# Second expert table read from the last column to the first, with PSUM written backwards

## The chip, the cores and the metric

The kernel runs on one core of one Trainium2 chip. The metric is the device time of one execution in microseconds, the median of several runs. TensorE (PE) multiplies, VectorE (DVE) and ScalarE (ACT) do elementwise work, GpSimd (POOL) helps with it, and SyncE (SP) issues the DMA transfers.

## The reference

One decoder layer over 256 tokens of width 1024. After two kinds of attention and an output projection, each token picks experts out of 16,384 by product keys; each expert is a single neuron with a row in the table `peer_u` and a row in the table `peer_v`:

```python
u = u_table[idx_c]
hid = jax.nn.gelu(jnp.einsum('cd,ced->ce', x_c, u), approximate=False)
return jnp.einsum('ce,ced->cd', g_c * hid, v_table[idx_c])
```

The result is added to the residual `h`. A last gate, `h + sigmoid(RMSNorm(h) @ W_g) * (p @ W_ple)`, gives the output.

## The kernel before, in words

The kernel doesn't gather rows of experts. It computes all 16,384 neurons for all 256 tokens as dense products, and the weights of the experts that a token didn't pick are zero. Each table goes through SBUF in 128 chunks of 128 experts x 1024 columns (512 KB), in a ring of four places (`RING`).

Products of fp32 accuracy are made of three products of a shorter format (fp32r): a tensor is split into a rounded part (`_hi`) and what is left (`_lo`), and hi x hi, hi x lo and lo x hi are summed in PSUM.

The first table's stage (about 185 to 577 us) makes the hidden values: `hidden` calls `three` (L1261 to L1263), whose output is 128 experts x 256 tokens. The second table's stage (about 577 to 927 us) is `expert_sum`, which the diff touches. For chunk n = 4i + q:

- SP loads the chunk into `t_raw` (L361) as soon as TensorE has raised `v_used` for the chunk that was in this place.
- ACT rounds it to `t_hi` (L613) and the gated hidden values `slots` to `g_hi` (L687).
- DVE subtracts, which gives `t_lo` (L964) and `g_lo` (L1144).
- TensorE multiplies. For two token tiles (`tt`) and two halves of 512 columns (`w`) it makes the three products L1597, L1599 and L1600, 12 in a chunk, and adds them up in the four PSUM banks 0 to 3 over all 128 chunks. The gates are the stationary operand, the table's rows the moving one.

The work of each engine is written out by hand in its own program, and the engines meet at semaphores. After the last chunk DVE adds the four banks to `h` (L1177), TensorE transposes `h` (L1248) and the last stage makes the gate with products of 512 and of 256 columns (L1640 to L1642).

Two other places bear on the prediction. `running_sum` (L1379 to L1384) has a product whose output leaves out every other 128 columns of a bank:

```python
mm(bank[3 * e + b][:, :].rearrange("p (i t) -> p i t", i=2)[:, :, P:SEQ], ones,
   upper[:, 256 * b:256 * (b + 1)].rearrange("p (i t) -> p i t", i=2), start=False,
```

and `biased` (L872) has DVE read an operand in SBUF from its last column to its first:

```python
in1=skew[:, a:b:2, 0:SEQ - s_from][:, :, ::-1], op0=ALU.mult, op1=ALU.add)
```

L1505 makes the key scores with plain f32 operands, which aren't split.

Of the kernel before, what the change touches and what calls it, by code (L numbers as in the profile page):

```python
# [72 lines left out]
def layer_program(nc, x, first, p_t, rel_bias, bucket_onehot, consts, qk_gain, w_in, w_out, w_query,  # L73
# [5 lines left out]
    with ctx:  # L79
# [11 lines left out]
        def tile(name, shape, offset, dt=f32):  # L91
            return nc.alloc_sbuf_tensor_at(name, shape, dt, offset=offset)
# [76 lines left out]
        t_lo = tile("t_lo", [P, RING, D], ZONE, f32r)  # L169
# [3 lines left out]
        g_hi = tile("g_hi", [P, RING, SEQ], ZONE + 4 * 4096, f32r)  # L173
        g_lo = tile("g_lo", [P, RING, SEQ], ZONE + 4 * 5120, f32r)
        t_hi = tile("t_hi", [P, RING, D], ZONE + 4 * 7168, f32r)
# [12 lines left out]
        bank = [pairs[b // 2][:, 2 * (b % 2):2 * (b % 2) + 2, :, :].rearrange("p a b c -> p (a b c)")  # L188
                for b in range(4)] + [ctx.enter_context(nc.psum_tensor(f"bank{b}", [P, 512], f32))
                                      for b in range(4, 8)]  # L190
# [3 lines left out]
        def xt_half(k, c):  # L194
            return half((4, 5, 6, 7)[c // 2] if k == 2 else (0, 1, 4, 5)[c // 2] if k == 1 else c // 2, c % 2)
# [82 lines left out]
        def u_lo(q, i):  # L278
            return t_lo_pool, RING * i + q + 1
# [964 lines left out]
        def _(pe):  # L1244
            mm = nc.tensor.matmul

            def transpose(src, tt, c, dst):
                return nc.tensor.transpose(dst, src[:, tt, P * c:P * (c + 1)], ident)  # L1248
# [57 lines left out]
            for c in range(DC):  # L1306
# [7 lines left out]
                for tt in range(TT):  # L1314
                    ins = mm(bank[4 + tt][:, :], xt_hi[:, c, P * tt:P * (tt + 1)], w_lo[:, 0, c, :], start=False,
                             stop=(c == DC - 1))
# [7 lines left out]
            for tt in range(TT):  # L1324
                ins = mm(bank[1][:, P * tt:P * (tt + 1)], neg_ones, diag[:, P * tt:P * (tt + 1)], start=True, stop=True)
# [8 lines left out]
            for g in range(8):  # L1334
                for tt in range(TT):
                    ins = nc.tensor.transpose(bank[g // 2][:, 256 * (g % 2) + P * tt:256 * (g % 2) + P * (tt + 1)],
                                              qk_nat[:, tt, 2 * g:2 * g + 2, :].rearrange("p a b -> p (a b)"), ident)
# [8 lines left out]
            for i in range(4):  # L1346
                if i >= 2:
                    pe.wait_ge(columns_out, 2 + i)
                for e in range(2):
                    r = slice(HD * e, HD * (e + 1))  # L1350
                    mm(bank[3 * e + i // 2][:, 256 * (i % 2):256 * (i % 2) + 256], qkt_s[r, 4 + i, 0:P], qkt_s[r, i, :],
                       start=(i % 2 == 0), stop=True, skip_group_check=True)
                for e in range(2):
                    r = slice(HD * e, HD * (e + 1))
                    ins = mm(bank[3 * e + 2][:, P * i:P * (i + 1)], qkt_s[r, 4 + i, P:SEQ], qkt_s[r, i, P:SEQ],
                             start=(i == 0), stop=True, skip_group_check=True)
# [41 lines left out]
            for hh in range(NH):  # L1398
# [3 lines left out]
                ins = nc.tensor.transpose(bank[weight_banks[hh // 4]][:, P * (hh % 4):P * (hh % 4 + 1)], s0[:, hh, :], ident)  # L1402
# [5 lines left out]
            for tt in range(TT):  # L1408
                for hh in range(NH):
                    e, i = hh % 2, hh // 2  # L1410
                    cols = slice(512 + HD * hh, 512 + HD * (hh + 1))
                    dst = bank[4 + tt][:, HD * hh:HD * (hh + 1)]
                    c = 256 * i + P * tt
                    ins = mm(dst, sb_w[:, e, c:c + P], v_all[:, 0, cols], start=True, stop=(tt == 0))
                    if tt:
                        ins = mm(dst, sb_w[:, e, 1024 + P * i:1024 + P * (i + 1)], v_all[:, 1, cols], start=False,
                                 stop=True)
# [3 lines left out]
            for hh in range(NH):  # L1421
                ins = mm(bank[2][:, HD * hh:HD * (hh + 1)], probs_t[:, hh // 4, P * (hh % 4):P * (hh % 4 + 1)],
                         v_all[:, 0, HD * hh:HD * (hh + 1)], start=True, stop=True)
# [3 lines left out]
            for hh in range(NH):  # L1427
                if hh % 4 == 0:
                    pe.wait_ge(s_exp, 3 + hh // 4)
                for ss in range(2):  # L1430
                    c = 256 * (hh % 2) + P * ss
                    ins = nc.tensor.transpose(bank[weight_banks[2 + hh // 2]][:, c:c + P], s1[:, hh, P * ss:P * (ss + 1)], ident)
# [10 lines left out]
            for hh in range(NH):  # L1443
# [5 lines left out]
                for ss in range(2):  # L1449
                    c = 256 * (hh % 2) + P * ss  # L1450
                    ins = mm(bank[3][:, HD * hh:HD * (hh + 1)], probs_t[:, place, c:c + P],
                             v_all[:, ss, HD * hh:HD * (hh + 1)], start=(ss == 0), stop=(ss == 1))
# [34 lines left out]
            for tt in range(TT):  # L1487
                pe.wait_ge(xs_ready, tt + 1)
                for c in range(DC):
                    ins = transpose(xs, tt, c, xt_half(2, c)[:, P * tt:P * (tt + 1)])  # L1490
# [53 lines left out]
            for q in range(2):  # L1544
                for tt in range(TT):
                    ins = nc.tensor.transpose(bank[q][:, P * tt:P * (tt + 1)], pick[:, tt, q, :], ident)
                ins.then_inc(pick_t_done, 1)
            pe.wait_ge(picks_ready, 1)
            for tt in range(TT):
                ins = nc.tensor.transpose(bank[2][:, P * tt:P * (tt + 1)],  # L1550
                                          gate[:, tt, :, :].rearrange("p a b -> p (a b)"), ident)
# [33 lines left out]
            def expert_sum(q, i, first=False, tiles=(0, 1)):  # L1585
                if 0 in tiles:
                    if first and q < LEAD:
                        pe.wait_ge(*u_lo(q, N_KEYS // RING))
                    else:
                        pe.wait_ge(t_lo_ready, RING * i + q - LEAD + 1)  # L1590
                    pe.wait_ge(g_lo_ready, RING * i + q + 1)
                for tt in tiles:
                    t = slice(P * tt, P * (tt + 1))
                    for w in range(2):
                        d = slice(512 * w, 512 * (w + 1))
                        dst = bank[2 * tt + w][:, :]
                        mm(dst, g_hi[:, q, t], t_hi[:, q, d], start=first and q == 0, stop=False,  # L1597
                           skip_group_check=True)
                        mm(dst, g_hi[:, q, t], t_lo[:, q, d], start=False, stop=False, skip_group_check=True)  # L1599
                        ins = mm(dst, g_lo[:, q, t], t_hi[:, q, d], start=False, stop=True,  # L1600
                                 skip_group_check=True)
                if 1 in tiles:
                    ins.then_inc(v_used, 1)
                return ins
# [10 lines left out]
            for q in range(RING):  # L1615
                expert_sum(q, 0, first=True)
            with pe.Fori(1, N_KEYS // RING - 1) as i:
                for q in range(RING):
                    expert_sum(q, i)
            for q in range(RING - 2):  # L1620
                expert_sum(q, N_KEYS // RING - 1)
            for q in range(RING - 2, RING):
                ins = expert_sum(q, N_KEYS // RING - 1, tiles=(0,))
# [6 lines left out]
            for u, (tt, d0, width, b) in enumerate(END_PARTS):  # L1630
                t, d = slice(P * tt, P * (tt + 1)), slice(d0, d0 + width)
                dst = bank[b][:, 0:width]
# [4 lines left out]
                for c in range(DC):  # L1637
                    if c % 2 == 0:
# [3 lines left out]
                    ins = mm(dst, xt_lo[:, c, t], wg_hi[:, c, d], start=False, stop=(c == DC - 1),  # L1642
                             skip_group_check=True)
# [66 lines left out]
```

## Time and profile before

| what | value |
|---|---|
| median of 3 runs | 954.15 us (953.89 to 954.45) |
| span of the profiled execution | 954.3 us |
| own time of the profiled execution | the page gives none beside the span |
| TensorE busy | 946.7 us (99%) |
| VectorE, ScalarE, GpSimd busy | 689.4, 614.5, 334.2 us |
| clock granted to TensorE | full in every slice |

The span reaches from the first to the last instruction of one execution. Busy times of TensorE count a product from its start to its modelled end, and products overlap, so that the distance from one start to the next says more of their price than their duration.

### The profile page before, as it was taken

Reading aid. Unit: us, or ns where it says so; the run is one execution under the profiler, and the core shown is the slowest. Engines: PE = TensorE matmul, PEld = TensorE weight load, DVE = VectorE, ACT = ScalarE, POOL = GpSimd, SP = SyncE. Lnnn points to the kernel's source line nnn. Section 1 sums busy time; section 2 is a strip of 40 time slices with the busy share of each in tenths; the row PEclk is TensorE's granted clock in tenths of the full one; section 3 lists DMA queues with packets and bytes.
Section 4 is the critical chain, followed back from the end, with each engine's and each line's share of the span. In section 5 each row is a group of like instructions: output and inputs, shape, how many; then the busy total and the mean of one; then the engine's idle time right before and its main releaser. Section 6 shows DMA issues by size and latency. Waiting matters only on the chain.

```text
span 954.3 us, 19175 instructions
## 1 busy us (share of the span) xinstructions
PE 946.7 (99%) x6220; PEld 863.2 (90%) x6220; DVE 689.4 (72%) x1389; ACT 614.5 (64%) x1039; POOL 334.2 (35%) x148
## 2 busy tenths in 40 slices
PE   9999999999999999999999999999999999999998
PEld 6988889999999999999999998888888888888887
DVE  6648864999987888889888875555555555566763
ACT  6778754456676888888888875544545554556643
POOL 0003500288887777777777772000000000000000
PEclk9999999999999999999999999999999999999999
DMA  9860453055555544444444445555567776655521
GB/s 335 305 257 1 156 214 133 24 177 185 189 180 175 175 161 170 163 167 158 172 160 170 164 167 196 185 193 197 197 229 236 239 244 222 195 197 191 188 105 45
DMA packets 46459, 172.08 MB, mean 180 GB/s; under 512 B 5043, under 2 KB 8668, under 8 KB 44892
## 3 DMA queue, kind: packets, MB, share of 16 engines
q1 hardware_dynamic: 46284, 171.53, 51.9%
q8 instruction: 19, 0.31, 0.1%
q10 hardware_dynamic: 144, 0.15, 0.1%
q14 instruction: 12, 0.10, 0.0%
HBM read 169.55 MB, written 2.11 MB: 180 GB/s over the span
## 4 chain that ended last, share of the span: by engine, by line
PE 88%; ACT 4%; DVE 3%; issue 2%; DMA 2%; POOL 1%; SPq 1%; DVEq 0%; ACTq 0%; POOLq 0%
PE bank L1262 12%; PE bank L1261 12%; PE bank L1263 12%; PE pair L1597 12%; PE pair L1600 12%; PE pair L1599 12%; PE pair L1558 3%; DMA h<-x 1%; PE pair L1295 1%; PE pair L1296 1%; PE pair L1297 1%; PE bank L1295 1%; PE bank L1297 1%; PE bank L1296 1%; PE bank L1642 1%
## 5 line engine op out<-in xcount | busy, mean ns | idle before, releaser
L613 ACT ACTIVATE t_hi<-t_raw 128x1024 fp32r<-128x1024 f32 x256 | 270.3, 1056 | 165.9 <-DMA t_raw<-v_chunks 162.5
L1233 POOL TENSOR_TENSOR t_lo<-t_raw,t_hi 128x1024 fp32r<-128x1024 f32 x130 | 311.9, 2411 | 147.0 <-ACT t_hi L613 147.0
L1262 PE MATMUL bank<-xt_lo,t_hi 128*128 128x256 f32 x1024 | 287.5, 281 | 0.0
L1261 PE MATMUL bank<-xt_hi,t_hi 128*128 128x256 f32 x1024 | 287.0, 280 | 0.2 <-POOL t_lo L1233 0.2
L1263 PE MATMUL bank<-xt_hi,t_lo 128*128 128x256 f32 x1024 | 286.5, 280 | 0.0
L964 DVE TENSOR_TENSOR t_lo<-t_raw,t_hi 128x1024 fp32r<-128x1024 f32 x126 | 154.4, 1226 | 136.5 <-ACT t_hi L613 136.3
L1597 PE MATMUL pair<-t_hi,g_hi 128*128 128x512 f32 x512 | 199.5, 390 | 0.3 <-DVE g_lo L1144 0.3
L1599 PE MATMUL pair<-t_lo,g_hi 128*128 128x512 f32 x512 | 199.2, 389 | 0.0
L1600 PE MATMUL pair<-t_hi,g_lo 128*128 128x512 f32 x512 | 199.2, 389 | 0.0
L1263 PEld LDWEIGHTS bank<-xt_hi,t_lo 128*128 128x128 f32 x1024 | 193.1, 189 | 0.0
L1261 PEld LDWEIGHTS bank<-xt_hi,t_hi 128*128 128x128 f32 x1024 | 192.8, 188 | 0.4 <-POOL t_lo L1233 0.4
L1262 PEld LDWEIGHTS bank<-xt_lo,t_hi 128*128 128x128 f32 x1024 | 192.4, 188 | 0.0
L1597 PEld LDWEIGHTS pair<-t_hi,g_hi 128*128 128x128 f32 x512 | 96.1, 188 | 20.9 <-DVE g_lo L1144 1.3
L1600 PEld LDWEIGHTS pair<-t_hi,g_lo 128*128 128x128 f32 x512 | 96.1, 188 | 20.0
L1599 PEld LDWEIGHTS pair<-t_lo,g_hi 128*128 128x128 f32 x512 | 96.1, 188 | 19.9
L1097 DVE TENSOR_SCALAR hot_j<-bank,pick_t 128x128 fp32r<-128x128 f32 x256 | 87.0, 403 | 0.0
L664 ACT ACTIVATE hot_j<-hot_j,ratio 128x128 fp32r<-128x128 f32 x256 | 82.1, 394 | 0.0
L677 ACT ACTIVATE bank<-bank 128x256 f32<-128x256 f32 x88 | 32.4, 368 | 39.8 <-PE bank L1263 33.1
L1113 DVE TENSOR_TENSOR slots<-slots,bank 128x256 f32 (+1 forms) x88 | 36.4, 414 | 28.7 <-ACT bank L677 28.7
L1144 DVE TENSOR_TENSOR g_lo<-slots,g_hi 128x256 fp32r<-128x256 f32 x128 | 54.4, 425 | 0.6 <-ACT g_hi L687 0.6
L687 ACT ACTIVATE g_hi<-slots 128x256 fp32r (+1 forms) x128 | 51.2, 400 | 0.6 <-DVE slots L1113 0.6
L1107 DVE TENSOR_TENSOR slots<-slots,pair 128x512 f32 (+1 forms) x64 | 44.1, 688 | 7.5
(285 smaller groups left out, 1286.5 us busy)
## 6 DMA issues: line engine op xcount, KB each, us to landing
t_raw<-u_chunks SPq DMA_DIRECT2D x128, 512.0 KB, 3.2
t_raw<-v_chunks SPq DMA_DIRECT2D x128, 512.0 KB, 3.3
w_raw<-w_query SPq DMA_DIRECT2D x4, 2048.0 KB, 8.1
w_raw<-w_in SPq DMA_DIRECT2D x3, 2048.0 KB, 10.4
w_raw<-w_out SPq DMA_DIRECT2D x2, 2048.0 KB, 8.2
wg_raw<-w_gate SPq DMA_DIRECT2D x8, 512.0 KB, 5.2
first_raw<-first SPq DMA_DIRECT2D x7, 384.0 KB, 7.0
w_raw<-w_in SPq DMA_DIRECT2D x4, 512.0 KB, 11.2
```

Of the source, the lines that this page charges most:

```text
L613: nc.scalar.activation(t_hi[:, q % RING, :], t_raw[:, q % RING, :], ACT.Copy).then_inc(t_hi_ready, 1)
L664: ins = nc.scalar.activation(hot_j[:, k, q, 1, :], hot_j[:, k, q, 0, :].bitcast(f32), ACT.Copy, scale=ratio[:, bass.ds(4 * s + q, 1)])
L964: nc.vector.tensor_tensor(t_lo[:, q % RING, :], t_raw[:, q % RING, :], t_hi[:, q % RING, :].bitcast(f32), ALU.subtract).then_inc(t_lo_read ...
L1097: nc.vector.tensor_scalar(hot_j[:, k, q, 0, :], lanes, pick_t[:, 1, bass.ds(t, 1)], pick_t[:, 2, bass.ds(t, 1)], ALU.is_equal, ALU.mult).t ...
L1144: nc.vector.tensor_tensor(g_lo[:, k, :], src, g_hi[:, k, :].bitcast(f32), ALU.subtract).then_inc(g_lo_ready, 1)
L1233: nc.gpsimd.tensor_tensor(t_lo[:, q, :], t_raw[:, q, :], t_hi[:, q, :].bitcast(f32), ALU.subtract).then_inc(t_lo_pool, 1)
L1261: mm(dst, ah, bh, start=(c == 0), stop=False)
L1262: mm(dst, ah, bl, start=False, stop=False)
L1263: ins = mm(dst, al, bh, start=False, stop=(c == n - 1))
L1597: mm(dst, g_hi[:, q, t], t_hi[:, q, d], start=first and q == 0, stop=False, skip_group_check=True)
L1599: mm(dst, g_hi[:, q, t], t_lo[:, q, d], start=False, stop=False, skip_group_check=True)
L1600: ins = mm(dst, g_lo[:, q, t], t_hi[:, q, d], start=False, stop=True, skip_group_check=True)
```

## The change

The three products of `expert_sum` take the columns of the table's half in descending order, and the output bank in descending order too. Each number is added at the same place of PSUM as before; only the order within a product is another.

```diff
                     for w in range(2):
                         d = slice(512 * w, 512 * (w + 1))
-                        dst = bank[2 * tt + w][:, :]
-                        mm(dst, g_hi[:, q, t], t_hi[:, q, d], start=first and q == 0, stop=False,
+                        dst = bank[2 * tt + w][:, ::-1]
+                        mm(dst, g_hi[:, q, t], t_hi[:, q, d][:, ::-1], start=first and q == 0, stop=False,
                            skip_group_check=True)
-                        mm(dst, g_hi[:, q, t], t_lo[:, q, d], start=False, stop=False, skip_group_check=True)
-                        ins = mm(dst, g_lo[:, q, t], t_hi[:, q, d], start=False, stop=True,
+                        mm(dst, g_hi[:, q, t], t_lo[:, q, d][:, ::-1], start=False, stop=False,
+                           skip_group_check=True)
+                        ins = mm(dst, g_lo[:, q, t], t_hi[:, q, d][:, ::-1], start=False, stop=True,
                                  skip_group_check=True)
```

## Rows read from the trace of the kernel before

**Rows 1.** The page: busy time of the engines; granted clock in 40 slices, in tenths.

```profile
PE 946.7 (99%) x6220; PEld 863.2 (90%) x6220; DVE 689.4 (72%) x1389; ACT 614.5 (64%) x1039; POOL 334.2 (35%) x148
...
PEclk9999999999999999999999999999999999999999
```

**Rows 2.** The page: the chain that ended last, by engine, by line.

```profile
PE 88%; ACT 4%; DVE 3%; issue 2%; DMA 2%; POOL 1%; SPq 1%; DVEq 0%; ACTq 0%; POOLq 0%
PE bank L1262 12%; PE bank L1261 12%; PE bank L1263 12%; PE pair L1597 12%; PE pair L1600 12%; PE pair L1599 12%; PE pair L1558 3%; DMA h<-x 1%; PE pair L1295 1%; PE pair L1296 1%; PE pair L1297 1%; PE bank L1295 1%; PE bank L1297 1%; PE bank L1296 1%; PE bank L1642 1%
```

**Rows 3.** The page's groups: busy us, mean ns | idle us before them.

```profile
L1597 PE MATMUL pair<-t_hi,g_hi 128*128 128x512 f32 x512 | 199.5, 390 | 0.3 <-DVE g_lo L1144 0.3
L1599 PE MATMUL pair<-t_lo,g_hi 128*128 128x512 f32 x512 | 199.2, 389 | 0.0
L1600 PE MATMUL pair<-t_hi,g_lo 128*128 128x512 f32 x512 | 199.2, 389 | 0.0
```

**Rows 4.** Timeline of TensorE, second table's stage: start us, duration us, line.

```profile
577.43 0.39 PE L1597 MATMUL pair<-t_hi,g_hi 128*128 128x512 f32 x1
...
700.55 0.39 PE L1597 MATMUL pair<-t_hi,g_hi 128*128 128x512 f32 x1
...
700.77 0.39 PE L1599 MATMUL pair<-t_lo,g_hi 128*128 128x512 f32 x1
...
701.00 0.39 PE L1600 MATMUL pair<-t_hi,g_lo 128*128 128x512 f32 x1
...
701.23 0.39 PE L1597 MATMUL pair<-t_hi,g_hi 128*128 128x512 f32 x1
...
925.13 0.38 PE L1248 MATMUL pair<-cst,h 128*128 128x128 f32 x2
...
925.92 0.47 PE L1597 MATMUL pair<-t_hi,g_hi 128*128 128x512 f32 x1
...
927.15 0.39 PE L1600 MATMUL pair<-t_hi,g_lo 128*128 128x512 f32 x1
```

**Rows 5.** Timeline of TensorE, last stage, two widths.

```profile
937.82 0.39 PE L1640 MATMUL bank<-wg_hi,xt_hi 128*128 128x512 f32 x1
...
939.63 0.39 PE L1642 MATMUL bank<-wg_hi,xt_lo 128*128 128x512 f32 x1
...
945.81 0.28 PE L1641 MATMUL bank<-wg_lo,xt_hi 128*128 128x256 f32 x1
...
946.89 0.28 PE L1641 MATMUL bank<-wg_lo,xt_hi 128*128 128x256 f32 x1
```

**Rows 6.** Timeline of TensorE, plain f32 key scores and what follows.

```profile
181.52 3.73 PE L1505 MATMUL pair<-sk,query 128*128 128x128 f32 x32
185.01 0.36 PE L1261 MATMUL bank<-xt_hi,t_hi 128*128 128x256 f32 x1
```

**Rows 7.** Timeline of TensorE, running sums.

```profile
80.09 0.28 PE L1381 MATMUL pair<-sp_hi,tri_r 128*128 128x256 f32 x1
80.20 0.40 PE L1379 MATMUL pair<-sp_hi,tri_r 128*128 128x512 f32 x1
80.43 0.28 PE L1381 MATMUL pair<-sp_hi,tri_r 128*128 128x256 f32 x1
80.55 0.40 PE L1384 MATMUL pair<-sp_hi,tri_r 128*128 128x512 f32 x1
```

**Rows 8.** Groups of DVE by line and shape, columns as in rows 3.

```profile
L927 DVE SCALAR_TENSOR_TENSOR h<-bank,stats,h 128x512 f32<-128x512 f32 x4 | 2.9, 746 | 0.1
...
L872 DVE SCALAR_TENSOR_TENSOR s<-bank,skew 128x512 f32<-128x512 f32 x4 | 2.6, 684 | 1.3 <-PE bank L1368 1.3
```

**Rows 9.** One stretch: its length; PE, PEld, DVE, ACT, POOL busy; clock, DMA share, GB/s.

```profile
660.00:780.00 120.00, 120.00 (x531) 99.41 (x530) 67.81 (x87) 60.00 (x88) 0.00 (x0) 1.00 0.67 227
```

**Rows 10.** Waits of SP's queue: total us, times, longest us.

```profile
SPq L361 <- PE pair L1600: 255.4, 124, 2.7
```

## The prediction

> **What bounds the kernel now.** I read the page's first part before anything else: TensorE is busy for 946.7 of 954.3 us, and its clock row grants full speed, 2.4 GHz, in all 40 slices [rows 1]. The chain of work that ended last says the same by another road: 88% of the span is TensorE, and three lines of the second table's loop, L1597, L1599 and L1600, hold 12% each, as the three lines of the first table do [rows 2]. So the second table's products are about 36% of the time by the chain, and the change edits these three lines and nothing else.
>
> Next I read that stage alone. The groups of instructions give 512 products of 128x512 on each line, 389 to 390 ns each [rows 3]. That duration is not the price of one: products overlap in the array. The price is the distance between starts. The timeline shows L1597, L1599 and L1600 and the next L1597 starting 0.22 to 0.23 us after each other, with no idle time noted before any of them [rows 4]. Over the stage, from the first L1597 at 577.43 to the last L1600 at 927.15, lie 349.7 us; the eight transposes of h that stand among the last products take 0.8 of them (925.13 to 925.92 in the timeline) [rows 4]. 348.9 us over 1,535 distances is 227.3 ns a product.
>
> What in those 227 ns depends on the columns? The last stage runs the same kind of product in two widths with hardly anything beside it: 512 columns start every 0.227 us (937.82 to 939.63 is 8 distances, 1.81 us), 256 columns every 0.120 us (945.81 to 946.89 is 9 distances, 1.08 us) [rows 5]. The difference, 107 ns for 256 columns, is 0.417 ns a column, one column for each beat of the 2.4 GHz clock; about 13 ns are left that no column pays for. The table stage therefore already runs at one column per beat: 213 + 14 = 227. It also runs at this pace while DMA, ACT and DVE are at work, as the last stage does almost alone, so nobody visibly disturbs its reads.
>
> **The change, part by part.** It removes no instruction, adds none, moves none and adds no wait. 128 table rows x 2 token tiles x 2 halves x 3 products = 1,536 products read their moving operand (t_hi or t_lo) from column 511 down to 0 and write the PSUM bank from 511 down to 0. Both reversed, each number lands where it did, so the DVE additions that read the banks afterwards, and the residual h, are untouched. The stationary operand (g_hi, g_lo) and its load are untouched as well. No queue changes order: DMA issues wait for v_used, which the last product of a row still raises.
>
> So there is one unknown: what a column costs when the addresses of a product go down. No row here shows a product that goes down, so I bound it. The lower bound is nothing: 0.417 ns a column stays, and 1,536 x 0 = 0. A gain would have to come out of the 13 to 14 ns beside the columns; all of it gone would be 1,536 x 13.3 ns = 20.4 us, and since a product of another stage pays the same 13 ns [rows 5] with other tiles, I see nothing in the order of columns that would free it. The upper bound comes from products that already cost more per column: the plain f32 scores of L1505. 32 records of 128 columns start between 181.52 and the next line's start at 185.01, which is 109 ns each, and with the 13 ns taken off 96 ns, 0.75 ns a column; taken with nothing off it is 0.85 [rows 6]. That is about two beats a column. Two beats for the reversed products would cost 512 x 0.417 = 213 ns more each, 1,536 x 213.3 ns = 327.7 us.
>
> The nearest rows favour the lower end. L1381 writes a bank in two runs with 128 columns left out between them, and it has the start distance of an unbroken 256-column product, 0.11 to 0.12 us [rows 7]; a break in the run is no cost by itself. And DVE already reads an operand from its last column to its first: L872 takes skew backwards and needs 684 ns for 512 columns, while L927, the same operation on as many columns going up, needs 746 [rows 8]. Both are neighbours only: the first still goes up inside each run, the second is another engine at more than 1 ns a column, which leaves its memory more time. I take zero for the sum, by the nearer row (same engine, same port), and keep 327.7 us as the other end.
>
> A rule speaks to this. The Trainium skill, "PSUM — Partial Sum Buffer", section Specifications (TRN2), says that PSUM is kept in lines of 8 bytes, two fp32 values, and that an access pattern which isn't contiguous slows matmuls a good deal. Read by the letter, a step of -1 isn't contiguous, and the sum would be the 327.7 us above or more; read by its lines, 511 and 510 share a line as 0 and 1 do, and the sum would be zero. Rows 7 don't decide it, since both runs there are made of whole lines.
>
> Nothing would hide a dearer column. TensorE has no idle time in this stage [rows 4], so every ns goes to the end. The others have room: in 120 us of the stage TensorE is busy for 120.0, DVE for 67.8, ACT for 60.0, DMA for 0.67 of the time [rows 9], and ACT waits for v rows only because the next load waits for TensorE to release a slot (SP's queue waited 255.4 us in total for L1600) [rows 10]. A dearer product gives them more room and changes no order.
>
> The sum: 954.3 + 0 = 954.3 us by the profiled span. The page gives no other time for that execution; the median of the runs is 954.15, 0.15 below, and I predict against it: 954.2. About 0.2%, some 2 us, is what a measurement of this kernel can tell from no change.
>
> **The rivals.**
>
> *Half rate (slower).* The two memories that a product touches hand over or take two fp32 columns in one access only if the second lies above the first; downward each column takes an access, and so two beats. Place: every one of the 1,536 products, in reading, in writing, or both at once (they run side by side, so both cost no more than one). Price: 327.7 us, so 954.2 + 327.7 = 1,281.9 us, and a start distance of 227 + 213 = 440 ns. It decides as soon as a column takes more than one beat. For it: the array takes a column each 0.417 ns and has no slack at all against its ports, so any lost pairing shows in full. Against it: rows 7 and 8. It is also where the letter of the rule in the Trainium skill's "PSUM — Partial Sum Buffer" would end.
>
> *A charge per product.* The descending start costs a bubble about as large as the 13 ns that a product already pays: 1,536 x 13.3 = 20.4 us, 974.6 us. For it: such a charge exists. Against it: L1381, whose starting address and shape differ from its neighbours', pays no more.
>
> *The change does nothing.* If the two reversals are cancelled when the program is put together, since reading and writing in either order is the same product, the time is 954.2 as well. It isn't told apart by the time, only by an experiment with one of them.
>
> **How the numbers follow.** No cost (with cancelled reversals): 0.54. Half rate: 0.36. Charge per product, or anything between it and half rate: 0.05. Four beats: 0.02. Faster: 0.03. The likeliest gives 954.2; its own range is 952.5 to 956. The whole range has to reach to half rate, for without it over 4 in 10 would be left out: 952 to 1,295, the upper end being 1,281.9 with 4% of the 327.7 for what lies beside the columns. Faster by over 0.2%: 0.03; within it: 0.54; slower: 0.36 + 0.05 + 0.02 = 0.43.
>
> **What would show it.** Right: the three lines still start every 227 ns, 349 us from first to last, and the chain gives each 12%. Half rate: starts 440 ns apart, the stage 677 us long, each line about 18% of a span of 1,282, with ACT's and DVE's waits in the stage growing and DMA's share falling by half. A charge: starts 240 ns apart. The prediction would be wrong through one thing only, the price of a descending column on one of TensorE's two ports; which port it is, the time doesn't say.

## The result, and the profile after

The changed kernel takes 964.62 us (median of 4 runs, 964.11 to 964.93) against 954.3 of before (4 runs): ratio 1.0102, 95% interval 1.0090 to 1.0114. It is slower by 10.3 us, about 1%; the number lies inside the stated range of 952 to 1,295 us only because that range had to reach as far as half rate; the likeliest value, 954.2, and its own range, 952.5 to 956, missed it.

First the page of the changed kernel: busy times, granted clock, chain by engine and by line. L1601 is the third product, which was L1600.

```profile
PE 955.8 (99%) x6220; PEld 864.0 (90%) x6220; DVE 678.2 (70%) x1389; ACT 616.1 (64%) x1039; POOL 334.6 (35%) x148
...
PEclk9999999999999999999999999999999999999999
...
PE 91%; ACT 3%; DVE 2%; issue 2%; POOL 1%; DMA 0%; POOLq 0%; ACTq 0%
PE pair L1601 12%; PE pair L1599 12%; PE pair L1597 12%; PE bank L1262 12%; PE bank L1261 12%; PE bank L1263 12%; PE pair L1558 3%; PE pair L1297 1%; PE pair L1295 1%; PE pair L1296 1%; PE bank L1295 1%; PE bank L1297 1%; PE bank L1296 1%; PE bank L1643 1%; PE bank L1641 1%
...
L1597 PE MATMUL pair<-t_hi,g_hi 128*128 128x512 f32 x512 | 203.5, 398 | 0.0
L1599 PE MATMUL pair<-t_lo,g_hi 128*128 128x512 f32 x512 | 203.5, 397 | 0.0
L1601 PE MATMUL pair<-t_hi,g_lo 128*128 128x512 f32 x512 | 203.5, 397 | 0.0
```

Nothing has changed its kind: the same number of instructions, full clock, the same bound, the same three lines with 12% each (answering to [rows 1, 2]). Only the products' duration has grown by 8 ns [rows 3]. The timeline of the changed kernel gives their distance:

```profile
576.87 0.40 PE L1597 MATMUL pair<-t_hi,g_hi 128*128 128x512 f32 x1
...
929.68 0.40 PE L1597 MATMUL pair<-t_hi,g_hi 128*128 128x512 f32 x1
...
933.65 0.40 PE L1601 MATMUL pair<-t_hi,g_lo 128*128 128x512 f32 x1
933.89 0.38 PE L1248 MATMUL pair<-cst,h 128*128 128x128 f32 x2
...
934.68 0.48 PE L1597 MATMUL pair<-t_hi,g_hi 128*128 128x512 f32 x1
...
935.93 0.40 PE L1601 MATMUL pair<-t_hi,g_lo 128*128 128x512 f32 x1
```

From 929.68 to 933.65 are 17 distances in 3.97 us: 233.5 ns, where before had 226 to 227 [rows 4]. The start times that the trace keeps to the nanosecond give 233.3 and 226.7. The stage lasts 935.93 - 576.87 = 359.1 us in place of 349.7. A view that counts products in a fixed stretch tells paces apart well; here it is for 600 to 900 us, before and after (length; PE, PEld, DVE, ACT, POOL busy with the number of instructions; clock, DMA share, GB/s):

```profile
600.00:900.00 300.00, 299.71 (x1322) 247.54 (x1321) 178.27 (x226) 155.94 (x226) 0.00 (x0) 1.00 0.62 210
```

```profile
600.00:900.00 300.00, 300.00 (x1287) 241.66 (x1286) 172.78 (x220) 151.06 (x220) 0.00 (x0) 1.00 0.60 204
```

300 us by 1,322 products is 226.9 ns, by 1,287 it is 233.1. (Such a quotient is rough to some 0.3 ns: the count takes in products that reach over an edge, and the stretch of before holds five longer distances, of 243 to 681 ns.) DVE and ACT do less in the stretch because they have fewer chunks to serve, and SP waits a little longer for TensorE:

```profile
SPq L361 <- PE pair L1601: 264.6, 124, 2.3
```

(255.4 before [rows 10]). So the loss is all in the distance between products: some 6.7 ns x 1,536 = 10.3 us. The spans of the two profiled executions differ by 8.8 us only. Here span and time can be compared: the changed kernel's profiled run took 964.77 us with a span of 963.1, and runs of the kernel before such as 954.56 us had a span of 952.8, so the execution behind the rows of before, with its span of 954.3, was itself some 1.5 us slower than the median.

### The profile page after: what moved, and what is told of

Read it like the earlier page. It is cut to its first block, busy times and chain, and to the rows that moved or that the text cites. A ratio compares the mean times of both kernels' runs of the same rounds, so it can differ in the third digit from the quotient of the medians.

```text
span 963.1 us, 19175 instructions
## 1 busy us (share of the span) xinstructions
PE 955.8 (99%) x6220; PEld 864.0 (90%) x6220; DVE 678.2 (70%) x1389; ACT 616.1 (64%) x1039; POOL 334.6 (35%) x148
## 4 chain that ended last, share of the span: by engine, by line
PE 91%; ACT 3%; DVE 2%; issue 2%; POOL 1%; DMA 0%; POOLq 0%; ACTq 0%
PE pair L1601 12%; PE pair L1599 12%; PE pair L1597 12%; PE bank L1262 12%; PE bank L1261 12%; PE bank L1263 12%; PE pair L1558 3%; PE pair L1297 1%; PE pair L1295 1%; PE pair L1296 1%; PE bank L1295 1%; PE bank L1297 1%; PE bank L1296 1%; PE bank L1643 1%; PE bank L1641 1%
## 5 line engine op out<-in xcount | busy, mean ns | idle before, releaser
L1262 PE MATMUL bank<-xt_lo,t_hi 128*128 128x256 f32 x1024 | 287.4, 281 | 0.0
L1261 PE MATMUL bank<-xt_hi,t_hi 128*128 128x256 f32 x1024 | 287.2, 280 | 0.2 <-POOL t_lo L1233 0.2
L1263 PE MATMUL bank<-xt_hi,t_lo 128*128 128x256 f32 x1024 | 286.5, 280 | 0.0
L1597 PE MATMUL pair<-t_hi,g_hi 128*128 128x512 f32 x512 | 203.5, 398 | 0.0
L1599 PE MATMUL pair<-t_lo,g_hi 128*128 128x512 f32 x512 | 203.5, 397 | 0.0
L1601 PE MATMUL pair<-t_hi,g_lo 128*128 128x512 f32 x512 | 203.5, 397 | 0.0
L1261 PEld LDWEIGHTS bank<-xt_hi,t_hi 128*128 128x128 f32 x1024 | 192.7, 188 | 0.4 <-POOL t_lo L1233 0.4
L1263 PEld LDWEIGHTS bank<-xt_hi,t_lo 128*128 128x128 f32 x1024 | 193.0, 189 | 0.0
L1262 PEld LDWEIGHTS bank<-xt_lo,t_hi 128*128 128x128 f32 x1024 | 192.5, 188 | 0.0
L1601 PEld LDWEIGHTS pair<-t_hi,g_lo 128*128 128x128 f32 x512 | 96.3, 188 | 23.3
L1599 PEld LDWEIGHTS pair<-t_lo,g_hi 128*128 128x128 f32 x512 | 96.3, 188 | 23.1
```

What stands on the lines that cost most here:

```text
L1261: mm(dst, ah, bh, start=(c == 0), stop=False)
L1262: mm(dst, ah, bl, start=False, stop=False)
L1263: ins = mm(dst, al, bh, start=False, stop=(c == n - 1))
L1597: mm(dst, g_hi[:, q, t], t_hi[:, q, d][:, ::-1], start=first and q == 0, stop=False, skip_group_check=True)
L1599: mm(dst, g_hi[:, q, t], t_lo[:, q, d][:, ::-1], start=False, stop=False, skip_group_check=True)
L1601: ins = mm(dst, g_lo[:, q, t], t_hi[:, q, d][:, ::-1], start=False, stop=True, skip_group_check=True)
```

## The experiments

Three theories after the result. D: a descending read costs 6.7 ns by itself. S: the cost lies between the last address of one product and the first of the next. W: it lies between the product's read of the table and the read of the stationary operand (the gates) for the next product. In a measured result the brackets hold the ratio to the kernel before, run beside it, and its 95% interval. In the two runs that turn only one of reading and writing, the host lays each half of the table out mirrored, so that the output stays the same.

**Which port?**

```diff
 read_down:   dst = bank[2 * tt + w][:, :]        t_hi[:, q, d][:, ::-1]   (t_lo alike)
 write_down:  dst = bank[2 * tt + w][:, ::-1]     t_hi[:, q, d]
+both:        v_chunks ... .reshape(N_KEYS, N_KEYS, 2, 512)[..., ::-1]
```

> Only the moving operand is read downward; the PSUM bank is written upward, and the table's halves are mirrored in memory beforehand so that the output is the same. Theory A (the 6.7 ns a product, 1,536 x 6.7 = 10.2 us, arise where the moving operand is read): 964.5 us, the three lines start every 233 ns. Theory B (they arise where PSUM is written): 954.3 us, 227 ns. Theory C (either one alone costs it, both side by side no more): 964.5 here and in the run that only writes downward.

> Only the PSUM bank is written downward, the operand is read upward (halves mirrored in memory). Theory A (reading): 954.3 us, 227 ns a product. Theory B (writing): 964.5 us, 233 ns. Theory C: 964.5.

Measured: 964.38 us (1.0101, 1.0084 to 1.0118) and 954.62 us (1.0001, 0.9992 to 1.0011). The same stretch of read_down, then of write_down:

```profile
600.00:900.00 300.00, 300.00 (x1287) 241.71 (x1286) 172.66 (x219) 151.09 (x220) 0.00 (x0) 1.00 0.60 205
```

```profile
600.00:900.00 300.00, 300.00 (x1325) 248.41 (x1324) 179.04 (x227) 155.92 (x226) 0.00 (x0) 1.00 0.61 211
```

The whole loss comes with the read; writing PSUM downward is free. The Trainium skill's rule that a PSUM pattern which isn't contiguous slows matmuls ("PSUM — Partial Sum Buffer", Specifications (TRN2)) doesn't hold by the letter for a step of -1: 1,325 products in the stretch against 1,322.

**Per product or per column?**

```diff
-                    for w in range(2):
-                        d = slice(512 * w, 512 * (w + 1))
-                        dst = bank[2 * tt + w][:, :]
+                    for w in range(4):
+                        d = slice(256 * w, 256 * (w + 1))
+                        dst = half(2 * tt + w // 2, w % 2)     # quarters_down: [:, ::-1], and t_hi, t_lo too
...                                                            # start only where w is even: two quarters share a bank
```

> Control, nothing downward: the same stage with products of 256 columns, 3,072 in place of 1,536. From rows 5 a 256-column product starts every 120 ns: 3,072 x 120 = 368.6 us in place of 1,536 x 227 = 348.7, so 954.3 + 20 = 974 us whatever the theory.

> The changed kernel with 256-column products, all downward. If the charge is one per product: 3,072 x 6.7 = 20.5 us above the control, about 995 us, starts 126.7 ns apart. If it is a charge per column (10.2 us over the same 786,432 columns): about 984.5 us, starts 123.3 ns apart.

Measured: up 974.96 us (1.0208), as expected; down 969.79 us (1.0157), 5.2 us faster than up, where both theories wanted it slower. The stretch of quarters_up, then of quarters_down:

```profile
600.00:900.00 300.00, 300.00 (x2503) 300.00 (x2502) 167.27 (x214) 146.74 (x213) 0.00 (x0) 1.00 0.58 199
```

```profile
600.00:900.00 300.00, 300.00 (x2534) 299.80 (x2533) 169.58 (x215) 148.29 (x216) 0.00 (x0) 1.00 0.60 202
```

119.9 ns up, 118.4 down. With 256 columns going down gains 1.5 ns, with 512 it loses 6.7. So there is neither a charge for a descending product nor one for a descending column that holds at both widths. What is left is that the 13 ns beside the columns are no constant.

**Where in the product?** middle_down reverses L1599 alone; blocks_down takes four runs of 128 columns in descending order and each run upward; runs_down leaves the runs in order and reverses each.

```diff
 middle_down: mm(dst[:, ::-1], g_hi[:, q, t], t_lo[:, q, d][:, ::-1], ...)     # the other two as before
 blocks_down: t_hi[:, q, d].rearrange("p (b c) -> p b c", b=4)[:, ::-1, :]      # t_lo and dst alike
 runs_down:   t_hi[:, q, d].rearrange("p (b c) -> p b c", b=4)[:, :, ::-1]
```

> Only the second product of each three (L1599, which reads t_lo) goes downward. Theory D (a descending read costs 6.7 ns by itself): the product that goes down takes 233 ns to the next start, the other two 227; 512 x 6.7 = 3.4 us, 957.9 us. Theory S (the cost lies at the change from one product's last address to the next one's first address): here a product that ended at column 511 is followed by one that starts at 511, and one that ended at 0 by one that starts at 0; neither pair stands in the kernel before or in the changed one, so the distances are neither 227 nor 233 and change at two of the three lines. Theory W (the read meets the next weights' read in SBUF): as D for this run.

> Each product takes its four runs of 128 columns in descending order, and each run upward. Theory D (a step of -1): 227 ns, 954.5 us. Theory S (last and first address): the product starts at column 384 and ends at 127, so the distance moves off 227, towards 233 if a start above the end is what costs. Theory W: no firm number; off 227 if the address in the first part of a product decides, since that is when the next weights are loaded.

> The four runs of 128 columns stand in ascending order, and each run goes downward. Theory D: the step of -1 costs at least as much as before, 233 ns or more, 964.5 us or more (four turns in place of one). Theory S: starts at 127 and ends at 384, near to the upward order, 227 ns, 954.5 us. Theory W: between, as the first run is read downward while weights are loaded.

Measured: 958.5 us (1.0038, 1.0024 to 1.0053), 955.23 us (1.0004, 0.9995 to 1.0014) and 965.2 us (1.0112, 1.0095 to 1.0129). The stretch of middle_down, blocks_down and runs_down:

```profile
600.00:900.00 300.00, 299.82 (x1308) 244.97 (x1307) 176.87 (x224) 154.14 (x225) 0.00 (x0) 1.00 0.60 208
```

```profile
600.00:900.00 300.00, 299.58 (x1322) 247.77 (x1321) 178.25 (x226) 156.00 (x227) 0.00 (x0) 1.00 0.60 210
```

```profile
600.00:900.00 300.00, 300.00 (x1285) 241.17 (x1284) 173.43 (x221) 151.07 (x220) 0.00 (x0) 1.00 0.60 205
```

One product of three reversed costs about a third, 3.9 us, and by the start times it is the reversed product's own distance to the next start that grows: L1599 takes 232 or 233 ns, the other two mostly 226 to 228. A product that starts at column 384 and ends at 127 costs nothing while its runs go up, and one that starts at 127 and ends at 384 pays in full when its runs go down. S is out: first and last address don't matter. The order inside a run does, and four descending runs cost no more than one of 512.

**Does the place of the gates matter?** The two gate tiles, which TensorE reads as the stationary operand, are moved by 128 or 64 bytes within the row of each partition; the tables stay.

```diff
-        g_hi = tile("g_hi", [P, RING, SEQ], ZONE + 4 * 4096, f32r)
-        g_lo = tile("g_lo", [P, RING, SEQ], ZONE + 4 * 5120, f32r)
+        g_hi = tile("g_hi", [P, RING, SEQ], ZONE + 4 * 4128, f32r)     # 64 bytes: 4112
+        g_lo = tile("g_lo", [P, RING, SEQ], ZONE + 4 * 5152, f32r)     #           5136
```

> The changed kernel with both gate tiles (the stationary operands) 128 bytes further on in SBUF; the table tiles stay where they are. Theory W (the descending read meets the weights' read in the same part of SBUF): the distance moves off 233 ns, in one direction or the other. Theories D and S know nothing of the weights: 233 ns, 964.5 us.

> The changed kernel with the gate tiles 64 bytes further on in place of 128. Theory W: the place of the weights sets the pace of the downward products, so that it is again another (226.7, 240 or a mixture; 954 to 975 us), and it may differ between executions as with 128 bytes (965.1 and 974.0 us). Theory D: 233.3 ns and 964.5 us in each execution.

> Control for the run with the gates 128 bytes further on: the same shift, all products upward. [...] Theory D (the step of -1 costs, the place of the weights doesn't): 226.7 ns, 954.5 us, and no execution with another pace.

Measured: 128 bytes, down, 965.08 us (1.0107, 1.0090 to 1.0124; five runs: 964.52, 964.82, 965.08, 967.22 and 974.04, of which 974.04 is the profiled one); 64 bytes, down, 965.09 us (1.0113); 128 bytes, up, 964.14 us (1.0102, 1.0085 to 1.0119). The last is the key run: nothing goes downward in it, and it loses as much as the change. The stretch of gates_shifted_down (its execution of 974.04 us), gates_shifted_64_down and gates_shifted_up:

```profile
600.00:900.00 300.00, 300.00 (x1251) 234.69 (x1250) 168.00 (x213) 147.56 (x214) 0.00 (x0) 1.00 0.57 199
```

```profile
600.00:900.00 300.00, 300.00 (x1288) 241.54 (x1287) 172.61 (x219) 151.08 (x220) 0.00 (x0) 1.00 0.60 204
```

```profile
600.00:900.00 300.00, 300.00 (x1291) 242.57 (x1290) 172.75 (x220) 152.04 (x221) 0.00 (x0) 1.00 0.61 205
```

Two timelines show two kinds of loss. First gates_shifted_down, where each product starts exactly 0.24 us after the last; then gates_shifted_up, where the distances are uneven, 0.23 and 0.24:

```profile
700.08 0.40 PE L1599 MATMUL pair<-t_lo,g_hi 128*128 128x512 f32 x1
700.32 0.40 PE L1601 MATMUL pair<-t_hi,g_lo 128*128 128x512 f32 x1
...
702.96 0.40 PE L1599 MATMUL pair<-t_lo,g_hi 128*128 128x512 f32 x1
```

```profile
700.32 0.39 PE L1599 MATMUL pair<-t_lo,g_hi 128*128 128x512 f32 x1
700.55 0.39 PE L1600 MATMUL pair<-t_hi,g_lo 128*128 128x512 f32 x1
...
701.47 0.40 PE L1597 MATMUL pair<-t_hi,g_hi 128*128 128x512 f32 x1
701.71 0.40 PE L1599 MATMUL pair<-t_lo,g_hi 128*128 128x512 f32 x1
701.95 0.39 PE L1600 MATMUL pair<-t_hi,g_lo 128*128 128x512 f32 x1
```

D said that the gates' place doesn't matter and is out as the whole story. W is left, though it risked little: for 128 bytes, down, it wanted a change either way, and for 128 bytes, up, it allowed one as well as none. Of the five downward executions only the profiled one lies far from the 964.5 us of D; the distances in the other four weren't recorded. For 64 bytes, down, it wanted another pace or a mixture. The mean stayed (300 us by 1,288), but the distances are a mixture: by the start times they take turns at 235 and at 231 or 232 ns, where the changed kernel has 233 or 234 throughout.

ACT and DVE write the gate tiles, so moving the tiles moved these writes too. A stretch of gates_shifted_down in which no engine but TensorE ran settles that, with two rows from inside it, a product and the load of the next stationary operand:

```profile
801.61:802.79 1.18, 1.18 (x6) 0.93 (x5) 0.00 (x0) 0.00 (x0) 0.00 (x0) 1.00 0.82 274
```

```profile
802.32 0.40 PE L1599 MATMUL pair<-t_lo,g_hi 128*128 128x512 f32 x1
802.32 0.19 PEld L1601 LDWEIGHTS pair<-t_hi,g_lo 128*128 128x128 f32 x1
```

The distances there are 240 ns as everywhere in this execution. From 600 to 900 us 42 of its distances lie wholly where VectorE, ScalarE and GpSimd had no instruction running, 228 where no DMA packet moved, and 11 where neither did; all are 240 ns, and of the first two kinds the changed kernel has 26 and 229, all 233 or 234. So the extra time doesn't need anyone else's access at that moment.

**Relative or absolute place?** The kernel before with every tile 128 bytes further on.

```diff
-        base = (nc.sbuf_base + 63) // 64 * 64
+        base = (nc.sbuf_base + 63) // 64 * 64 + 128
```

> The kernel before, all products upward, with every tile in SBUF 128 bytes further on: gates and tables move together, so that only their absolute place is new. If the gates' place against the tables' place sets the pace (theory W, relative): 226.7 ns, 954.5 us. If the gates' absolute place does (a row of weights that no longer lies where it did against some boundary): about 232.7 ns, 964 us, as with the gates alone 128 bytes further on.

Measured: 954.73 us (1.0003, 0.9994 to 1.0013), in the stretch:

```profile
600.00:900.00 300.00, 299.77 (x1323) 247.87 (x1322) 178.27 (x226) 156.03 (x227) 0.00 (x0) 1.00 0.61 210
```

The gates may lie 128 bytes further on if the tables do too. What counts is the place of the one against the other, not where both lie.

**Other stages downward.** The second table goes up again; the first table's products and the last stage's read and write downward.

```diff
-                three(hid_bank(q), [(..., (xt_hi[:, c, :], xt_lo2[:, c, :])) for c in range(DC)]
+                three(hid_bank(q)[:, ::-1], [(..., (xt_hi[:, c, ::-1], xt_lo2[:, c, ::-1])) for c in range(DC)]
-                    mm(dst, xt_hi[:, c, t], wg_hi[:, c, d], ...)
+                    mm(dst[:, ::-1], xt_hi[:, c, t], wg_hi[:, c, d][:, ::-1], ...)     # the other two alike
```

> The second table's stage goes upward as before; the first table's products (256 columns, three each 117.5 ns apart in the mean) and the last stage's go downward. Theory D (6.7 ns per downward product): 3,072 x 6.7 + 72 x 6.7 = 21 us more, 975.5 us, and the 512-column products of the last stage, with hardly any other engine at work, 233 ns apart. Theory W: the first table's distance moves off 117.5 either way (112 to 124 by what stands in the trace of before and of the 256-column runs), 938 to 975 us; the last stage's as its own tiles lie.

Measured: 957.76 us (1.0029, 1.0015 to 1.0044), not 975. The timeline of its last stage, and the stretch with its 512-column products, in which DMA has little to do (a share of 0.13, against 0.60 in the second table's stage), while ACT and DVE work on:

```profile
937.03 0.40 PE L1640 MATMUL bank<-wg_hi,xt_hi 128*128 128x512 f32 x1
...
947.30 0.40 PE L1642 MATMUL bank<-wg_hi,xt_lo 128*128 128x512 f32 x1
947.53 0.28 PE L1640 MATMUL bank<-wg_hi,xt_hi 128*128 128x256 f32 x1
...
952.03 0.28 PE L1642 MATMUL bank<-wg_hi,xt_lo 128*128 128x256 f32 x1
```

```profile
937.03:947.53 10.50, 10.50 (x46) 8.46 (x45) 4.67 (x13) 6.08 (x11) 0.00 (x0) 1.00 0.13 50
```

44 distances in 10.27 us are 233.4 ns with 512 columns (226 before [rows 5]), and 38 distances in 4.50 us are 118.4 with 256 (120 before). Both numbers are those of the second table's stage, with other tiles and little DMA traffic. The first table's products barely moved in the mean: from 190 to 290 us this kernel holds 840 of them where the kernel before holds 848, and from 310 to 560 us 2,127 where before (the second row) holds 2,130:

```profile
310.00:560.00 250.00, 250.00 (x2127) 250.00 (x2126) 219.78 (x492) 208.40 (x451) 187.10 (x80) 1.00 0.49 165
```

```profile
310.00:560.00 250.00, 250.00 (x2130) 250.00 (x2129) 220.20 (x492) 208.85 (x453) 188.85 (x80) 1.00 0.48 166
```

But each line did move, and the moves cancel: by the start times of this second stretch L1261's mean distance to the next start went from 117.5 to 121.9 ns, L1262's from 117.6 to 115.2, L1263's from 117.5 to 115.9.

No run is faster than the kernel before.

## Why the prediction was wrong in its main point

**Bound and cover: right.** The stage was TensorE's alone, nothing hid a dearer product, and the 6.7 ns went to the end one for one: 6.7 ns x 1,536 is the 10.3 us measured.

**The price of a descending column: right as far as it went.** No run shows a dearer column; 0.417 ns a column stays, and half rate and four beats, 38 chances in 100 together, are far off. Writing downward costs nothing. The reading that priced half rate was wrong besides: L1505's 109 ns are no price of its 128 columns. In the same trace plain f32 records of 64 columns take as long, 16 of them in the 1.73 us between these two rows, 108 ns each:

```profile
97.49 1.90 PE L1451 MATMUL pair<-v_all,probs_t 128*128 128x64 f32 x16
99.22 1.04 PE L1248 MATMUL bank<-cst,o_nat 128*128 128x128 f32 x8
```

**The step that failed** is "I take zero for the sum, by the nearer row", and under it the reading of the 13 to 14 ns beside the columns. I took them for a fixed charge because two stages paid the same, and asked only whether a column would cost more. They are no such charge: they depend on how the product's two tiles lie and in which order the columns are read: 13.3 ns upward, 20.0 downward, 26.7 downward in the execution with the gates moved, and with 256 columns 13.3 upward and about 12 downward (distances less 0.417 ns a column). The trace of before already held a row against a fixed charge: the first table's 256-column products start 117.4 ns apart (250 us by 2,130), those of the last stage 120 [rows 5]; in the first table's stage one moving tile, `xt_lo2`, starts 128 bytes off the rest, though no run tests whether that is why. That two stages paid the same fits this: by the layout the tiles of both start at the same place modulo 512 bytes, and the last stage, too, pays 6.7 ns more when it goes downward.

**The rival "a charge per product"** had the right shape for this change, at 5 chances in 100 together with all between it and half rate, and twice the size: 13.3 for 6.7 ns. Its mechanism, a bubble for a descending start, is refuted: blocks_down starts high and is free, four descending starts in runs_down cost no more than one, and 256-column products gain by going down.

**"I see nothing in the order of columns that would free it"**, of the 13 ns, was too firm as well: 256 columns downward do give back 1.5 ns.

**Rows 7 and 8** were no neighbours for this question. Rows 7 go upward inside each run, which is what turned out to be free in blocks_down too; rows 8 are an engine that doesn't load a stationary operand beside its read.

Shown: the loss is in the read, inside the runs; it depends on direction, width and the gates' place against the table's; and it is as large over products beside which no other engine runs. Concluded, not seen: that it is the load of the stationary operand that meets the read. The load is the one user of the gate tiles left once their writers stand still, and it starts within a few ns of the product before it; but its recorded time is the same 188 ns at 226.7, 233.3 and 240.0 ns, so the rows show no wait in it. How the two get in each other's way, and why one program ran at 965 and at 974 us, stays open.

## What to carry to other kernels

The time that a stream of products needs beside its columns was no constant here: moving one operand's tile by 128 bytes against the other's cost this kernel 1%, as much as reading backwards did. When a layout change moves the time of a TensorE-bound stage by a few ns per product, measure the distance between starts first, and move the tiles against each other before blaming the edit itself. A pattern with a step of -1 in PSUM was free here; a price that holds at one width need not even have the same sign at another.

## What was not expected of the hardware

The distances of 512-column products came in steps: 226.7, 233.3 and 240.0 ns, 6.7 ns or 16 columns apart, each kept over the stretch of the run where it appeared, a few longer distances of the kernel before apart (1,322, 1,287 and 1,251 products in 300 us). Other runs fall into patterns. In gates_shifted_up the same seven distances, from 228 to 241 ns, come round again and again up to about 798 us, 232.4 ns in the mean; from 800 us on, in the same execution, distances of 229 or 230 and of 237 or 238 take turns, 233.3 in the mean. Seven products fit neither the three lines nor the 12 products of a chunk, and the tiles lie as they did when the pattern changes. So the place of the tiles isn't all that sets a pace: the pattern that the stream happens to be in counts too, and what holds or changes it, no run here shows. The Trainium skill ("TensorE: Matmul & The Clock Gate", Back-to-back issue gap) says that in a real kernel the spacing of products is set by the weight load and the product together. The runs here agree in kind, since the place of the stationary operand alone moved the spacing from 226.7 to 232.7 ns in the mean of the start times; the figure that it gives for 512 columns, about 131 ns, isn't met by any row of these kernels.
